# The gates of the second transformer type in three reduced-precision passes, with their input kept as two parts

## The reference, cut to what matters

```python
def mixer_block(x, w_in, ...):
    p_swa, p_rwkv, p_fox, p_dsa, p_gate = split_cols(x @ w_in, IN_GROUPS)
    o_swa = swa_branch(...)      # windowed attention
    o_rwkv = rwkv7_branch(...)   # a recurrence over tokens, done in chunks
    o_fox = fox_branch(...)      # causal attention with a forget gate
    o_dsa = dsa_branch(...)      # attention on keys chosen by a top-k
    gates = sigmoid(p_gate.reshape(B, S, 4, D_MODEL) + gate_bias)
    merged = sum(gates[:, :, i] * (o_i @ w_i) for the four branches)
    return merged @ w_out

def second_block(x, ...):
    for layer in range(2):
        x = layer_norm(ALPHA * x + mixer_block(x, ...), ...)
        y = swiglu(x) if layer == 0 else moe(x)
        x = layer_norm(ALPHA * x + y, ...)
```

## Time and profile before

| | |
|---|---|
| median of three runs | 2494.39 us |
| profiled execution | 2499.6 us |
| its span, first to last instruction | 2497.8 us |
| TensorE busy | 2397.1 us, 96% of the span |
| VectorE busy | 1529.6 us, 61% |
| ScalarE busy | 1090.7 us, 44% |
| mean granted TensorE clock | 0.984 |

### The profile page before, as it was taken

One profiled execution on the slowest core, in us unless ns is written; L12 is line 12 of the kernel. 1 busy time (PEld: TensorE's weight loads), 2 busy tenths in 40 slices (PEclk: granted clock), 3 DMA queues, 4 the chain that ended last, 5 costly groups with the idle time before them and its releaser, 6 DMA issues.

```text
span 2497.8 us, 41012 instructions
## 1 busy us (share of the span) xinstructions
PE 2397.1 (96%) x15617; PEld 1990.0 (80%) x15617; DVE 1529.6 (61%) x3424; ACT 1090.7 (44%) x2009; POOL 0.2 (0%) x4
## 2 busy tenths in 40 slices
PE   7998999999988999999999899999999999999998
PEld 3854678888884899998788899897788788778885
DVE  4567453333477765666575866856746655558893
ACT  3236343223236654543212545542304554557882
POOL 0000000000000000000000000000000000000000
PEclk9999999999999999999999999999999999999999
DMA  8236522332325656562334465543332655359997
GB/s 333 91 118 235 168 85 93 99 95 93 93 85 191 199 173 182 185 186 81 97 99 117 144 200 186 160 149 101 98 91 77 239 190 175 136 207 352 333 357 270
DMA packets 182499, 409.85 MB, mean 164 GB/s; under 512 B 20256, under 2 KB 20512, under 8 KB 181792
## 3 DMA queue, kind: packets, MB, share of 16 engines
q1 hardware_dynamic: 182304, 407.23, 50.2%
HBM read 406.10 MB, written 1.05 MB: 163 GB/s over the span
## 4 chain that ended last, share of the span: by engine, by line
PE 86%; DVE 9%; ACT 1%; issue 1%; DMA 1%; SPq 0%; DVEq 0%; ACTq 0%
PE bank L853 11%; PE bank L856 11%; PE bank L857 11%; PE bank L1167 9%; PE bank L1184 6%; PE bank L1188 5%; PE bank L1187 5%; PE bank L815 4%; PE bank L873 2%; PE bank L876 2%; PE bank L877 2%; PE bank L1094 2%; PE bank L1008 2%; PE bank L1142 2%; PE bank L1319 1%
## 5 line engine op out<-in xcount | busy, mean ns | idle before, releaser
L2520 DVE TENSOR_TENSOR WL<-ring,WH 128x512 fp32r<-128x512 f32 x632 | 414.0, 688 | 234.6 <-ACT WH L1746 232.9
L1746 ACT ACTIVATE WH<-ring 128x512 fp32r<-128x512 f32 x632 | 375.8, 624 | 294.7 <-PE bank L853 199.5
L2605 DVE TENSOR_TENSOR WLE<-slots,WHE 128x1024 fp32r<-128x1024 f32 x231 | 281.4, 1224 | 122.9 <-ACT WHE L1746 119.2
L1746 ACT ACTIVATE WHE<-slots 128x1024 fp32r<-128x1024 f32 x231 | 244.6, 1061 | 114.8 <-PE bank L1184 113.9
L853 PE MATMUL bank<-AH,WH 128*128 128x256 f32 (+1 forms) x832 | 268.0, 322 | 11.9 <-DVE WL L2520 8.1
L856 PE MATMUL bank<-AL,WH 128*128 128x256 f32 (+1 forms) x832 | 267.5, 322 | 0.0
L857 PE MATMUL bank<-AH,WL 128*128 128x256 f32 (+1 forms) x832 | 265.6, 319 | 0.0
L1167 PE MATMUL bank<-X,ring 128*128 128x256 f32 x1024 | 249.6, 391 | 0.0
L1167 PEld LDWEIGHTS bank<-X,ring 128*128 128x128 f32 x1024 | 189.3, 191 | 35.8 <-issue 7.3
L853 PEld LDWEIGHTS bank<-AH,WH 128*128 128x128 f32 x832 | 159.9, 192 | 26.1 <-issue 9.5
L857 PEld LDWEIGHTS bank<-AH,WL 128*128 128x128 f32 x832 | 158.8, 191 | 12.1
(11 more groups left out here) (419 smaller groups left out, 4803.0 us busy)
## 6 DMA issues: line engine op xcount, KB each, us to landing
ring<-stream SPq DMA_DIRECT2D x992, 256.0 KB, 2.8
slots<-experts SPq DMA_DIRECT2D x264, 512.0 KB, 5.2
con<-consts SPq DMA_DIRECT2D x1, 2884.0 KB, 13.4
X<-xin SPq DMA_DIRECT2D x1, 2048.0 KB, 9.4
par<-params SPq DMA_DIRECT2D x1, 1302.5 KB, 6.9
LAST<-final_rows SPq DMA_DIRECT2D x1, 1024.0 KB, 4.8
out<-ZO SPq DMA_DIRECT2D x4, 256.0 KB, 2.0
con<-consts SPq DMA_DIRECT2D x1, 132.0 KB, 2.7
```

The costliest lines, as they stand in the source:

```text
L1746: return nc.scalar.activation(o, i, fn, **kw)
L2520: V.tensor_tensor(WL[:, s % SPLIT, :], ring[:, c % RING, :], WH[:, s % SPLIT, :].bitcast(F32), ALU.subtract).then_inc(w_taken, 1)
L2605: V.tensor_tensor(WLE[:, s % PAIR_SPLIT, :], pair(pair_of(s)), WHE[:, s % PAIR_SPLIT, :].bitcast(F32), ALU.subtract).then_inc(pair_taken, 1)
```

## The change

The gate blocks are multiplied in the three passes. Their chunks hold gate blocks alone now, 64 per layer, and are split by ACT and DVE like the others. The branch chunks stay whole; each run of them begins a chunk of its own, which makes 24 chunks per layer for 80 blocks. The order of PE's work, counted in gate blocks and tiles, is as it was.

DVE's new `gate_low` makes the low parts. It is called in `take`, for the gate blocks that stand on PE ahead of the next tile after the one taken (and no more than 4 chunks past those that had begun when the taken tile began), and in attention for the blocks of the next step. ACT's `gate_high` follows each kept gate and runs up to five chunks ahead of it.

The input x is kept as two parts, `XRN` (in the place of `X`) and `XL`, in place of x, `PH` and `PL`. The residual after the output projection adds both parts, which takes two DVE instructions. The copy of x to `X` in norm 6 goes. In `early_norm` the low parts of weights are made at more and other places, two more chunks of them before the correction of the first tiles, and the feed-forward that follows takes one more chunk ahead in each of its early steps.

```diff
@@ tensor engine
             def gates(n):
...
-                    ins = pe.matmul(o, weight(st["n"]), X[:, kk, 0:T], start=kk == 0, stop=kk == KD - 1)
+                    k, at = divmod(st["gate"], CHUNK)
+                    c = split_index(gate_chunk(k))
+                    wh, wl = (W[:, c % SPLIT, at * P:(at + 1) * P] for W in (WH, WL))
+                    if at == 0:
+                        pe.wait_ge(w_taken, c + 1)
+                    ins = pe.matmul(o, wh, XRN[:, kk, :], start=kk == 0, stop=False)
+                    if at == 0:
+                        ins.then_inc(split_begun, 1)
+                    read_signal(pe.matmul(o, wh, XL[:, kk, :], start=False, stop=False))
+                    ins = pe.matmul(o, wl, XRN[:, kk, :], start=False, stop=kk == KD - 1)
@@ scalar engine
+                    gate_high(l, 2 * (p + 1) + SPLIT - 1)
...
+            def gate_high(l, k):
+
+                high_to(GATE_CHUNKS[l][min(k, len(GATE_CHUNKS[l])) - 1] + 1)
@@ scalar engine, early_norm
-                    if j < KD - 1:
+                    if ni in (3, 5) and j < KD - 1:
                         act.wait_ge(early_used, (KD - 1) * (ni - EARLY[0]) + j + 1)
...
-                if ni >= 6:
-                    x_written(ni, bias)
+                high_to(after + 14)
@@ vector engine
+            def gate_low(blocks, begun):
+
+                upto = min(-(-blocks // CHUNK), -(-begun // CHUNK) + SPLIT - 2)
+                while st["gate"] < upto:
+                    c = gate_chunk(st["gate"])
+                    s = split_index(c)
+                    dve.wait_ge(w_hi, s + 1)
+                    V.tensor_tensor(WL[:, s % SPLIT, :], ring[:, c % RING, :], WH[:, s % SPLIT, :].bitcast(F32),
+                                    ALU.subtract).then_inc(w_taken, 1)
+                    st["gate"] += 1
+
             def take():
 
+                u = st["u"]
+                gate_low(unit_blocks[min(u + 1, len(unit_blocks) - 1)], unit_blocks[u])
                 dve.wait_ge(gemm_done, st["u"] + 1)
...
@@ vector engine, early_norm
-                early_kept(ni, u0, 0, dsts[:2])
                 for j in range(KD):
+                    if j % 2 == 0:
+                        early_kept(ni, u0, j // 2, dsts[j // 2:j // 2 + 1])
                     low_to(after + 9 + j // 2)
-                    if j == KD // 2:
-                        early_kept(ni, u0, 2, dsts[2:])
...
+                low_to(after + 14)
                 early_centred(ni, u0, 0, dsts, finals)
@@ vector engine, feed-forward
                     low_to(c0 + value_chunks(q) + AHEAD)
+                    if q < tiles_early:
+                        low_to(c0 + gate_chunks(tiles_early) + AHEAD + q + 1)
@@ vector engine
+            def residual_joined(j, b):
+
+                link(V.scalar_tensor_tensor(X[:, j, 0:T], XRN[:, j, :].bitcast(F32), ALPHA, b, ALU.mult, ALU.add))
+                return V.scalar_tensor_tensor(X[:, j, 0:T], XL[:, j, :].bitcast(F32), ALPHA, X[:, j, 0:T], ALU.mult, ALU.add)
```

More of the change, by code:

```diff
@@ L292, in stream_plan @@
         wide(w, (l,), C_FOX + 512, 2)
-        gates = [(i, j, kk) for i, j in PAIRS for kk in range(KD)]
-        branches = list(PAIRS)
+        gate_blocks = [(w, (l,), kk * P, C_GATE + i * D + j * P, P) for i, j in PAIRS for kk in range(KD)]
+        gate_at, pair = 0, 0
+        gate_chunks_of.append([])
+        branch_chunks_of.append([])
         for kind, n in mixer_fill():
             if kind == "gate":
-                for i, j, kk in gates[:n]:
-                    blocks.append((w, (l,), kk * P, C_GATE + i * D + j * P, P))
-                gates = gates[n:]
-            else:
-                for i, j in branches[:n]:
-                    tiles("w_branch_2", (l,), [j * P], BR_K[i], sum(BR_K[:i]) * P)
-                branches = branches[n:]
+                for _ in range(n):
+                    if gate_at % CHUNK == 0:
+                        gate_chunks_of[l].append(len(blocks) // CHUNK)
+                        blocks += gate_blocks[gate_at:gate_at + CHUNK]
+                    gate_at += 1
+                continue
+            run = [("w_branch_2", (l,), (sum(BR_K[:i]) + kk) * P, j * P, P) for i, j in PAIRS[pair:pair + n] for kk in range(BR_K[i])]
+            pair += n
+            branch_chunks_of[l] += range(len(blocks) // CHUNK, (len(blocks) + len(run) + CHUNK - 1) // CHUNK)
+            blocks += run
+            pad()
         pad()
@@ L323, in stream_plan @@
     pad()
-    return blocks, starts, projections
+    return blocks, starts, projections, gate_chunks_of, branch_chunks_of
 def build(nc, stream, experts, params, consts, xin, final_rows, out):
@@ L797, in _ @@
         def _(pe):
-            st = dict(n=0, u=0, a=0, t=0, g=0, s=0, h=0, ada=0, p=0, alo=0, free=0, ready=0, gate=0)
+            st = dict(layer=0, branch=0, n=0, u=0, a=0, t=0, g=0, s=0, h=0, ada=0, p=0, alo=0, free=0, ready=0, gate=0)
             def weight(n):
@@ L824, in unit_begin @@
                 u = st["u"]
+                unit_blocks.append(st["gate"])
                 if u >= BANKS:
@@ L970, in split_tok_tiles @@
             def split_tok_tiles(tiles, n, apart=False):
-                hi, lo = (PHN, PLN) if apart else (PH, PL)
+                hi, lo = (XRN, XL) if apart else (PH, PL)
                 units = [unit_begin()[:, 0:n * P] for _ in range(tiles)]
@@ L1109, in attention @@
                     early(p)
+                    if kind == "second":
+                        step_blocks.append(st["gate"])
                     if 1 <= p <= pairs:
@@ L1177, in branches @@
                 for i, j in PAIRS[st["p"]:st["p"] + n]:
-                    tile(lambda kk: CAT2[:, sum(BR_K[:i]) + kk, :], BR_K[i], T)
+                    b = unit_begin()
+                    for kk in range(BR_K[i]):
+                        k, at = divmod(st["branch"], CHUNK)
+                        c = BRANCH_CHUNKS[st["layer"]][k]
+                        if at == 0:
+                            pe.wait_ge(w_loaded[c % RING], 16 * (c // RING + 1))
+                        mm(b[:, 0:T], ring[:, c % RING, at * P:(at + 1) * P], CAT2[:, sum(BR_K[:i]) + kk, :],
+                           kk == 0, kk == BR_K[i] - 1, kk == BR_K[i] - 1)
+                        st["branch"] += 1
+                        st["free"] += at == CHUNK - 1
+                if st["branch"] % CHUNK:
+                    st["branch"] += -st["branch"] % CHUNK
+                    st["free"] += 1
                 st["p"] += n
@@ L1568, in _ @@
             for l in range(2):
+                st["layer"], st["branch"] = l, 0
+                st["free"] += 1
                 early_group(4 + 2 * l)
@@ L1786, in early_norm @@
                 else:
+                    high_to(after + 3)
                     for j in range(KD):
@@ L1959, in ffn_part @@
                     high_to(c0 + gate_chunks(q) + AHEAD)
+                    if early and q < EARLY_TILES // 2:
+                        high_to(c0 + gate_chunks(EARLY_TILES // 2) + AHEAD + q + 1)
                     if early and q < EARLY_TILES // 2:
@@ L2179, in _ @@
                     return
[L2180 removed]
+                early_norm(6, XRN, lambda j, s: pr("ln2b_0", j, j + 1), pr("eps5"), **tail)
         @block.vector
@@ L2185, in _ @@
             V = nc.vector
-            st = dict(u=0, a=0, g=0, tmp=0, chain=0, c=0, h=0, p=0, pair=0)
+            st = dict(u=0, a=0, g=0, tmp=0, chain=0, c=0, h=0, p=0, pair=0, gate=0, step=0)
             def link(ins):
@@ L2457, in attention @@
                 for s in range(len(us)):
+                    if kind == "second" and s % 2 == 0:
+                        at = st["step"] + s // 2
+                        gate_low(step_blocks[at + 1], step_blocks[at])
                     if diff:
@@ L2488, in attention @@
                 normalise(len(us) - 1)
+                if kind == "second":
+                    gate_low(step_blocks[st["step"] + pairs + 1], step_blocks[st["step"] + pairs])
+                    st["step"] += pairs + 2
                 copy_out(pairs - 2)
@@ L3419, in pair_slot, with gate_chunk @@
     return s if s < RING - 1 else s + 1
+def gate_chunk(k):
+    return (GATE_CHUNKS[0] + GATE_CHUNKS[1])[k]
 def split_index(c):
-    return c - sum(hi - lo for lo, hi in WHOLE if lo < c)
+    return c - sum(n < c for n in WHOLE_SET)
 def kernel(**inputs):
```

54 lines of the change are left out of this document (29 added, 25 removed).

## The result

| | before | changed |
|---|---|---|
| median of 4 runs, us | 2496.47 | 2565.15 |
| lowest and highest, us | 2489.43, 2499.11 | 2551.89, 2574.74 |
| span of the profiled execution, us | 2497.8 | 2573.0 |
| mean granted clock of it | 0.984 | 0.963 |

What follows compares the result with a forecast made beforehand. PE's pace bounds the kernel (96% of the span), with DVE as full in the top-k and rwkv's preparation; 46 + 10 - 4 = 52 us on 2499.6, less 5.2 for the median, gives 2546, range 2515 to 2582.

Steps and rivals of the forecast that it cites:

- Parts 2 and 3: DVE's 64 new low parts per layer, 42 us, come only after its earlier work: 46 us for two layers.
- Part 4: PE's granted clock falls behind five standstills of 4 us or more per layer: +10 us, none 0, all 16.
- Part 3: First layer's mixer stage by stage, doubled: low parts come late or are hidden; 22.8 us per layer, 46 for two.
- windowed attention: First attention: 12 low parts, 7.9 us, make DVE bound its steps: +2.4 us per layer, bounds 0 and +7.9.
- top-k: PE stands 7.5 us at the first gates; fox scores begin some 9 us late: +9.0, bounds +3.2 and +11.
- preparation: Rwkv's preparation: PE waits for low parts behind DVE's own work, first level 16.2 us late: +16.2, bounds +10 and +20.
- Part 1: PE's gate blocks: three passes save 0.08 us each, 40 us for 512, only where nothing else is late.
- Part 5: Early norms and residual: 5.41 us wait removed, second residual instruction delays the norm: -4 us together, bounds -10 and +5.
- (a): The pace decides, low parts are ready in time: 2449 us, or 2472 with half of the gain; 4%.
- (b): DVE makes up for the standstills where it idles and the clock stays up: 2513 us; 10%.
- (c): All low parts on the path, attention and levels bound by DVE too, through ACT's high parts: 2584 us; 12%.
- (d): No narrower product on PE: the triple takes as long as the float32 block: 2566 us; 4%.

Runs made afterwards that it cites:

- nearly free low parts: The changed kernel with GpSimd writing only 8 of 512 columns of each gate low part and DVE none: 2473.5 us, 0.9914 of the kernel before.
- short low parts at the old place: The changed kernel with each DVE gate low part writing 8 of 512 columns, same place, waits and signal: 2538.9 us, 1.0184 of the kernel before.
- the order alone: The kernel before with only the change's order of low parts in early norms and feed-forward; gates, residual and x as before: 2489.1 us, 0.9984.

## Why the prediction was right, and where its terms were off

Stage by stage, differences to before in us; in the last column the clock is held in most places (idle products in the standstills and the scan). The second attention of before is no even base: its clock falls too, to a mean of 0.92 in the first layer, where it takes 41.5 us, and not in the second, where it takes 38.2. PE's longest wait in that stage of the first layer is 0.40 us, at its start (1197.78 in the earlier trace rows), and yet the clock is at its lower level in a window like this one:

```profile
1204.30:1207.70 3.40, 3.40 (x11) 2.36 (x12) 0.65 (x5) 0.70 (x3) 0.00 (x0) 0.50 0.32 77
```

The forecast of 2546 lies 19 us below the 2565 measured; of the 17 us by which its 52 fall short of the 68.7, about 7 are in Parts 2 and 3 and about 9, by the ratios, in Part 4. Within Part 3 the stages are off by up to 2.5 us each and of both signs, which cancels in part.

| stage | forecast | changed, layers 1, 2 | clock held, layers 1, 2 |
|---|---|---|---|
| windowed attention | +2.4 | -0.2, -0.2 | -0.1, -0.2 |
| top-k | +9.0 | +13.9, +13.4 | +10.1, +10.1 |
| second attention | -3.2 | -4.6, +1.7 | -3.1, -2.9 |
| preparation | +16.2 | +21.4, +21.4 | +18.5, +18.6 |
| levels and scan | -3.4 | -1.7, +4.4 | -1.7, -1.9 |
| end | +1.8 | +3.8, +3.0 | +3.7, +2.0 |
| sum | +22.8 | +32.6, +43.8 | +27.4, +25.7 |

- **Part 1, the pace,** right in size: 0.08 us a block wherever PE is the bound. The 40 us never came in full: even with nearly free low parts it is 20, from 139 of the 256 blocks of a layer.
- **Parts 2 and 3, the new work and its place,** right in mechanism and nearly in size: 46 us forecast, 53 with the clock held. The two standstills in the top-k were forecast at 7 and 4 us and are 7.49 and 4.93; the two in the preparation at 7 and 9, and are 6.77 and 8.75, with a third of 4.08 ahead of the last 13 blocks, to which the forecast gave no length. The one at the end is 3.51 us. It is the order, not the load: short low parts at the old place still leave 33 us of waits a layer, full ones written earlier 8.8.
- **Windowed attention,** too high by 2.6, but right in kind: DVE is busy for only 28.5 of 35.4 us, yet with short low parts the stage takes 32.2. The 3.5 us that the blocks save there are used up by DVE's low parts, and no more than that.
- **Part 4, the clock,** is the term that was mis-sized: +10 (0 to 16) forecast; 19 by the ratios of the changed kernel (1.0288) and of the one with the clock held (1.0213), whose interval of 8 to 30 leaves room for the 10; and 23 by the stages of the two profiled executions. The step that failed is what was counted: five standstills of 4 us or more a layer, and nothing else. The top-k and the preparation, which hold the ten standstills above 4 us, account for 13 of the 23 us, 1.3 each where the forecast had 1.6. The other 10 lie in the second attention, the scan and the end, almost all in the second layer. PE waits there for 0.3 us at most in the attention, 1.26 in the scan and 3.51 at the end: the trace shows a fall among such waits too, though not each time, and 16 and 17 us at 0.50 with PE busy. The price of 1.6 was itself read short. The earlier trace rows end where the window ends, not where the fall does; the next 2.5 us of before are at 0.50 as well:

```profile
1427.00:1429.50 2.50, 2.50 (x14) 2.50 (x14) 1.29 (x2) 0.89 (x3) 0.00 (x0) 0.50 0.75 203
```

That would be 2.9 us a standstill; that 1.6 came out near is luck in part. The four executions of the changed kernel also stand in the order of their mean clock: 2551.89 us at 0.973, 2562.77 at 0.968, 2567.53 at 0.966 and, the profiled one, 2574.74 at 0.963. The Trainium skill ("TensorE: Matmul & The Clock Gate", Why this matters for your kernels) warns of idle gaps between bursts; the rows here show falls behind short waits as well, down to the 0.40 us above.
- **Part 5, norms and residual,** -4 forecast for norms and residual together, -4.0 (-8.5 to +0.5) measured for the order alone, so the sum of the two is not shown. The reason given was wrong: the 5.41 us wait shrank to 3.94, and a new one of 0.83 stands ahead of it. The residual is hidden in a difference: from the out-projection to the norm's product it is 35.4 us before, 33.9 with the order alone and 36.4 in the changed kernel. So up to 2.5 us in the first layer are the residual and what else differs there, within the 0.5 to 3 of the forecast. The profiles agree: between the mixers, at the slower of two paces told below, the order alone takes 312.4 us and the changed kernel 317.6.
- **The rivals.** (a) is excluded by the waits of 40.0 us in the first layer, (b) by the stages: nothing was made up outside the second attention, and the clock did not stay up. (c), everything on the path, has a number (2584) as far from the 2565 measured as the forecast's 2546. It has a part in the truth: in the first attention the low parts use up the whole saving, in the levels with the scan of the first layer 3.3 of 5.0 us. But they cost no more than the saving there, and the way through ACT's high parts is excluded, since these stand in the kernel with nearly free low parts too, whose first attention takes 32.0 us. (d), no narrower product, is excluded by the 5.0 us that the levels save.

## What to carry to other kernels

Before a product is made narrower by work on another engine, look in the windows for the stages where that engine is already full, and in the order for what stands ahead of the new work: the price is set there, not by the sum of its instructions. Price a wait of PE not only by its length: look at what the granted clock does in the stretch behind it, above all where small products follow. The saving of a faster product counts only in the stages where PE is the bound: here neither in the top-k nor in the preparation.

## What the runs showed of the hardware

The clock's fall behind a wait of 1.26 us and, in the kernel before, without any longer than 0.40, and its staying down for 17 us with PE busy, are told above; so is DVE's 1.75 us for 0.69 beside a working GpSimd. The third is new: two stretches of the feed-forward run at one of two paces at a granted clock of 1.00 in both. The same three-pass products behind norm 5, before, 45 products from the first row to the second, 5.10 us:

```profile
1444.25 0.28 PE L853 MATMUL bank<-AH,WH 128*128 128x256 f32 x1
...
1449.35 0.28 PE L853 MATMUL bank<-AH,WH 128*128 128x256 f32 x1
```

and changed, 45 products, 5.30 us:

```profile
1469.09 0.28 PE L864 MATMUL bank<-AH,WH 128*128 128x256 f32 x1
...
1474.39 0.28 PE L864 MATMUL bank<-AH,WH 128*128 128x256 f32 x1
```

0.1133 or 0.1178 us a product, 6 us over a stretch of 150. Of the 14 profiled executions 5 had the slower pace in the first such stretch (900 to 1030 us) and 4 in the second (1450 to 1590), in all four combinations. The changed kernel's profile had fast, slow, the other slow, fast: by the estimate of 6 us that is most of the 8.5 us which it seemed to gain ahead of the mixers and of the 6.8 it lost between them. Between the mixers at the same pace, the other versions of the change with the faster one take 311.4 to 313.7 us against 310.8 before. What decides it stays open. Both paces occur in the first stretch among kernels that are the same up to there, so it is no effect of the change, and two single profiles can differ by 12 us through it.
